# Attention and output projection of a band-attention layer, woven into one stage

## The chip, the core and the metric

One core of one Trainium2 chip runs the whole layer in one launch. The metric is the device time of that launch in microseconds (us). Engines that matter here: TensorE (PE: matmuls, and its weight loads, PEld), VectorE (DVE), ScalarE (ACT), GpSimd (POOL) and the DMA queues, nearly all of them issued by SyncE (SP). Each engine works through its own list of instructions in order; semaphores tie the lists together.

## The reference

All data is float32. 2048 prompt frames and 8 streams of 16 frames are projected by one matrix. One half of the channels goes through a gated MLP, the other through banded attention: 8 heads of 64 channels, queries in chunks of 64, each seeing its own chunk and the 8 before it, with a learned bias by clipped distance. Both halves are gated, multiplied by `w_out`, added to the input and normalised.

```python
def _band_attn_prompt(q, k, v, rel_table):
    ...
    scores = jnp.einsum('bnqhd,bnkhd->bnhqk', qc, kb).astype(jnp.float32) * (HEAD_DIM_B ** -0.5) + bias[None, None]
    scores = jnp.where(valid[None, :, None, None, :], scores, -jnp.inf)
    p = jax.nn.softmax(scores, axis=-1).astype(v.dtype)
    o = jnp.einsum('bnhqk,bnkhd->bnqhd', p, vb)
...
def _merge(x, a_out, z_a, b_out, z_b, w_out, g, bb):
    y = jnp.concatenate([a_out * jax.nn.silu(z_a), b_out * jax.nn.silu(z_b)], axis=-1)
    out = jnp.einsum('bse,ed->bsd', y, w_out)
    return _layernorm(ALPHA * x + out, g, bb)
```

## The kernel before

It has three stages, one after the other, with an end-of-block meeting of all engines between them.

1. **Input projection** (until about 700 us of the trace). The change leaves it alone but for small things named below. Each product is three float32r matmuls (high x high, high x low, low x high), which are nearly as exact as float32.
2. **Attention** (`attention`). The 2048 frames are 16 tiles of 128 queries. The outer loop runs over 4 pairs of heads, the inner over the 16 tiles: 64 units. A deep tile (number 4 and up, 12 of 16) sees 640 keys, which is 5 key tiles; tile 0 sees 1, tile 1 sees 2, and so on. A unit is a chain over three engines: PE makes the **scores** of both heads (L996; the low and high parts of a key stand on the two halves of the 128 rows, so two matmuls do a head's product); DVE adds the bias and finds the row's extreme (L921, one for each head); ACT takes the exponent and the row sum (L864); DVE **normalises** (reciprocal L928, scaling L930); PE **turns** the 128x128 blocks (L1006) into one of three PSUM banks; ACT copies them out (L872); PE **weighs** the values (L1019); DVE gates the sum (L940) into a store. PE's list has, at tile t, the scores of t, the weighing of t-2 and the turning of t-1. Meanwhile POOL splits `w_out` into its high and low parts, 8 pieces of 128x1024 (cast L854, subtraction L856), two for each pair of heads.
3. **Output projection** (`output_projection`). For each of 17 tiles of 128 rows (16 of the prompt, one of the 8 streams' frames): the gated activations come back from DRAM, ACT takes the high part (L1216), DVE the low part (L1255), PE makes two halves of 512 columns of 24 matmuls each (L1356), DVE adds the residual and takes statistics (L1264, L1267, L1273), POOL takes the root (L1203, L1205), DVE centres and scales (L1276, L1282), and the tile is stored. The 8 streams' small attention is threaded in, one stream every two tiles (L1365 to L1384).

Everything that PE writes has a bank of its own in stage 3: four banks for the output halves.

## Time and profile before

| | us |
|---|---|
| median of 3 runs | 1170.11 (1166.11 to 1170.15) |
| profiled execution, its own time | 1168.34 |
| its span, first to last instruction | 1166.3 |
| PE busy in the span | 1112.8 (95%) |
| stage 2 on PE, 704.2 to 956.4: PE busy | 221.3 of 252.2 |
| stage 3 on PE, 956.4 to 1158.8: PE busy | 201.7 of 202.4 |

The span is what the trace covers; the run's own time is 2.0 us longer, and the median of the runs another 1.8 us. PE's busy time counts each matmul until its modelled end, and matmuls overlap: how fast PE works is read from the distance of their starts. A row of the timeline has start, duration, engine, line, operation, what it writes and reads, and how many instructions are merged.

### The profile page before, as it was taken

Reading aid. Unit: us, or ns where it says so; the run is one execution under the profiler, and the core shown is the slowest. Engines: PE = TensorE matmul, PEld = TensorE weight load, DVE = VectorE, ACT = ScalarE, POOL = GpSimd, SP = SyncE. Lnnn points to the kernel's source line nnn. Section 1 sums busy time; section 2 is a strip of 40 time slices with the busy share of each in tenths; the row PEclk is TensorE's granted clock in tenths of the full one; section 3 lists DMA queues with packets and bytes.
Section 4 is the critical chain, followed back from the end, with each engine's and each line's share of the span. In section 5 each row is a group of like instructions: output and inputs, shape, how many; then the busy total and the mean of one; then the engine's idle time right before and its main releaser. Section 6 shows DMA issues by size and latency. Waiting matters only on the chain. (4 is left out here: it accounts for less than half of the span.)

```text
span 1166.3 us, 19127 instructions
## 1 busy us (share of the span) xinstructions
PE 1112.8 (95%) x6792; PEld 982.2 (84%) x6792; DVE 508.5 (44%) x1060; ACT 331.5 (28%) x690; POOL 93.4 (8%) x114
## 2 busy tenths in 40 slices
PE   6999999999999999999999995989898989999997
PEld 5999999999899999999999994878787877777775
DVE  4400112022222232222223225888888865665655
ACT  4411111111111111111111113768686761111110
POOL 0000000000000000000000010220202001111111
PEclk9999999999999999999999996999999999999999
DMA  8561111011342343244234339978787806545541
GB/s 275 184 193 64 55 38 56 26 66 43 120 155 81 109 148 115 93 139 144 76 109 152 110 97 226 272 193 197 188 197 179 198 29 201 164 127 158 161 135 72
DMA packets 127939, 155.81 MB, mean 134 GB/s; under 512 B 9097, under 2 KB 89121, under 8 KB 127905
## 3 DMA queue, kind: packets, MB, share of 16 engines
q1 hardware_dynamic: 123584, 139.63, 41.0%
q10 hardware_dynamic: 4320, 15.73, 4.2%
q8 instruction: 20, 0.33, 0.1%
q14 instruction: 15, 0.11, 0.0%
HBM read 101.56 MB, written 56.91 MB: 136 GB/s over the span
## 5 line engine op out<-in xcount | busy, mean ns | idle before, releaser
L601 PE MATMUL bank<-xh,wh 128*128 128x384 f32 (+1 forms) x1120 | 404.9, 362 | 9.4 <-DVE xl L487 7.9
L601 PE MATMUL bank<-xh,wl 128*128 128x384 f32 (+1 forms) x1120 | 401.1, 358 | 0.0
L601 PE MATMUL bank<-xl,wh 128*128 128x384 f32 (+1 forms) x1120 | 400.5, 358 | 0.0
L601 PEld LDWEIGHTS bank<-xh,wh 128*128 128x128 f32 x1120 | 211.0, 188 | 28.4 <-issue 9.1
L601 PEld LDWEIGHTS bank<-xh,wl 128*128 128x128 f32 x1120 | 210.8, 188 | 18.3
L601 PEld LDWEIGHTS bank<-xl,wh 128*128 128x128 f32 x1120 | 211.0, 188 | 17.5
L864 ACT ACTIVATE prob<-prob,low 128x640 f32<-128x640 f32 (+4 forms) x128 | 96.7, 756 | 66.2 <-DVE low L921 65.8
L1356 PE MATMUL out_ps<-wo_h,yh 128*128 128x512 f32 x272 | 109.5, 403 | 1.6 <-DVEq L1251 1.6
L1356 PE MATMUL out_ps<-wo_h,yl 128*128 128x512 f32 x272 | 106.3, 391 | 0.0
L1356 PE MATMUL out_ps<-wo_l,yh 128*128 128x512 f32 x272 | 106.1, 390 | 0.0
L514 DVE SCALAR_TENSOR_TENSOR st_b<-st_b,bank 128x384 f32<-128x384 f32 (+1 forms) x40 | 24.3, 607 | 181.0 <-ACT st_b L432 108.7
L1019 PE MATMUL o_ps<-pt,v 128*64 128x128 f32 x1120 | 77.5, 283 | 21.5 <-DVE st_b L940 14.4
L921 DVE CUSTOM_DVE_ANT_0 prob<-s_ps,bias 128x640 f32<-128x640 f32 (+4 forms) x128 | 90.0, 736 | 13.7 <-PE s_ps L996 10.6
L996 PE MATMUL s_ps<-k,q 128*128 128x320 f32 (+2 forms) x448 | 85.7, 331 | 8.3 <-DMA k<-s_k 8.2
L1019 PEld LDWEIGHTS o_ps<-pt,v 128*64 128x64 f32 x1120 | 61.7, 139 | 36.3 <-DVE st_b L940 16.8
L482 DVE TENSOR_TENSOR wl<-raw,wh 128x1024 fp32r<-128x1024 f32 x29 | 35.4, 1221 | 125.5 <-ACT wh L371 125.5
L567 DVE SCALAR_TENSOR_TENSOR st_b<-bank,st_a 128x384 fp32r<-128x384 f32 (+1 forms) x40 | 24.4, 611 | 144.2 <-ACT st_a L454 144.2
L930 DVE TENSOR_SCALAR prob<-prob,rden 128x640 f32<-128x640 f32 (+4 forms) x128 | 77.2, 603 | 4.5
L872 ACT ACTIVATE pt<-pt_ps 128x512 f32<-128x512 f32 (+1 forms) x168 | 75.8, 512 | 7.9 <-PE pt_ps L1006 7.8
L1006 PE MATMUL pt_ps<-ident,prob 128*128 128x128 f32 x560 | 77.6, 285 | 0.0
L996 PEld LDWEIGHTS s_ps<-k,q 128*128 128x128 f32 x448 | 68.8, 195 | 10.0 <-DMA k<-s_k 8.9
L1006 PEld LDWEIGHTS pt_ps<-ident,prob 128*128 128x128 f32 x560 | 62.4, 145 | 11.3 <-issue 11.3
(115 smaller groups left out, 818.0 us busy)
## 6 DMA issues: line engine op xcount, KB each, us to landing
raw<-w_all ACTq DMA_DIRECT2D x30, 512.0 KB, 3.3
q<-s_q SPq DMA_DIRECT2D x60, 256.0 KB, 6.0
par<-x SPq DMA_DIRECT2D x17, 512.0 KB, 3.3
big<-s_y SPq DMA_DIRECT2D x16, 512.0 KB, 5.3
y_out<-r SPq DMA_DIRECT2D x16, 512.0 KB, 3.1
k<-s_k SPq DMA_DIRECT2D x30, 256.0 KB, 7.2
big<-s_va SPq DMA_DIRECT2D x17, 256.0 KB, 3.3
big<-s_gate SPq DMA_DIRECT2D x17, 256.0 KB, 3.5
```

The source lines that it names most:

```text
L482: nc.vector.tensor_tensor(wl[s][:], raw[s][:], wh[s][:].bitcast(f32), ALU.subtract).then_inc(w_ready, 1)
L514: nc.vector.scalar_tensor_tensor(out=st, in0=st, scalar=1.0, in1=bank[c][:, 0:n], op0=ALU.add, op1=ALU.mult).then_inc(evac[c], 1)
L567: nc.vector.scalar_tensor_tensor(out=st_b[e % 2][:, 0:n].bitcast(f32r), in0=bank[c][:, 0:n], scalar=QSCALE if kind == "q" else 1.0, in1=st ...
L601: last = nc.tensor.matmul(bank[c][:, 0:width], w[s][:, kc, :], xx[:, kc, t0:t0 + width], start=kc == 0 and a == 0, stop=kc == KC - 1 and a ...
L864: nc.scalar.activation(prob[s][:, 0:n], prob[s][:, 0:n], ACT.Exp, bias=low[:, s:s + 1], scale=-1.0, accum_out=den[:, s:s + 1]).then_inc(ex ...
L872: nc.scalar.activation(pt[t % 2][:, 4 * e:4 * e + m, :], pt_ps[(BANKS[t] + e) % 3][:, 0:m, :], ACT.Copy).then_inc(pt_copied, 1)
L921: nc.vector.tensor_tensor_reduce(out=out, in0=src, in1=b, scale=1.0, scalar=MASKED, op0=ALU.add, op1=ALU.min, accum_out=low[:, s:s + 1]).t ...
L930: nc.vector.tensor_scalar(prob[s][:, 0:n], prob[s][:, 0:n], rden[:, s:s + 1], None, ALU.mult).then_inc(normed, 1)
L996: last = nc.tensor.matmul(s_ps[h][:, b, 0:m], q[:, h, part, t * P:(t + 1) * P], k[:, h, k0 + at:k0 + at + m], start=part == 0, stop=part == 1)
L1006: last = nc.tensor.transpose(pt_ps[(BANKS[t] + e) % 3][:, i - 4 * e, :], prob[(2 * t + h) % 4][:, b * P:(b + 1) * P], ident[:])
L1019: last = nc.tensor.matmul(o_ps[64 * h:64 * h + 64, 0:P], v[:, t + 1 - nk + b, 64 * h:64 * h + 64], pt[t % 2][:, 2 * b + h, :], start=b == ...
L1356: last = nc.tensor.matmul(out_ps[2 * s + h][:], y[s][:, c, :], w[:, c, 512 * h:512 * h + 512], start=c == 0 and a == 0, stop=c == KC - 1 a ...
```

## The change

Stages 2 and 3 become one stage, `attention_and_output`, written out in full (no loops). Its list is a sequence of 72 units: tile 0 with pairs 0 to 3, then stream 0, then tile 1 with its four pairs, then stream 1, and so on; from tile 8 on there are no streams left and a tile is four units. 81 steps run over it. In step s PE issues the scores of unit s, the turning of unit s-1 (first two groups of blocks), a **quarter** of a finished tile's output matmuls (12 of 48, in two lots of 6 with the third group of blocks between them), and the weighing of unit s-1. A tile's gating is one step after its last weighing, the high and low parts of its activations are taken in the same step, and its quarters follow. No quarter stands in steps 0 to 5 and in steps 10, 15, 20, 25, 30, 35 and 40; the stream tile is the ninth to be projected. The last 9 steps have no attention.

What else changes with it:

- The scores of a head pair are 12 matmuls instead of 8: three products (high x high, high x low, low x high), each over the 64 rows of its head alone, the two heads on rows 0 to 63 and 64 to 127 one after the other. Keys sit in a ring of 6 tiles, so 640 columns are two runs, of 384 and 256 or 512 and 128 columns.
- Turning has two PSUM banks instead of three, the output one bank (the very last half another) instead of four.
- Centring and scaling of 15 of the 17 output tiles go from two DVE instructions to three POOL instructions (L1025, L1028, L1030 of the new kernel). The last two tiles keep DVE's.
- The gated attention sums stay in SBUF, and gating is one instruction for a tile instead of four.
- The bias is loaded for all heads at the start of the stage (1.3 MB; before, the first 0.65 MB came during stage 1 and 0.65 MB more for each pair); queries are loaded once, not twice.
- POOL splits `w_out` in one run from the start of the stage.

```diff
+def output_schedule(order):
+    split, quarters, ends = [], {}, []
+    for k, tile in enumerate(order):
+        at = max(gate_step(tile), split[-1] if split else 0, ends[k - 2] + 1 if k > 1 else 0)
+        start = max(at + 1, ends[-1] + 1 if ends else 0)
+        for j in range(4):
+            quarters[start + j] = (k, j // 2, j % 2)
...
-                    for b, at, m in halves:
-                        for part in range(2):
-                            last = nc.tensor.matmul(s_ps[h][:, b, 0:m], q[:, h, part, t * P:(t + 1) * P],
-                                                    k[:, h, k0 + at:k0 + at + m], start=part == 0, stop=part == 1)
+                for first, count, at in runs:
+                    for i, (a, c) in enumerate(((0, 0), (0, 1), (1, 0))):
+                        for h in range(2):
+                            rows = slice(HD * h, HD * h + HD)
+                            last = nc.tensor.matmul(s_ps[h][:, at:at + count * P], q[t % 2][rows, a * GRP + p, :],
+                                                    k[rows, c * GRP + p, first * P:(first + count) * P],
+                                                    start=i == 0, stop=i == 2)
...
+            pool.wait_ge(par_loaded, 32)
+            for n in range(TILES):
+                root(n)
+                if n < POOL_TILES:
+                    pool.wait_ge(rstd_ready, n + 1)
+                    nc.gpsimd.tensor_scalar(r[n % 2], r[n % 2], mv[n % 2][:, 0:1], rstd[n % 2][:],
+                                            ALU.subtract, ALU.mult).then_inc(centred, 1)
+                    pool.wait_ge(centred, n + 1)
+                    nc.gpsimd.tensor_tensor(r[n % 2], r[n % 2], gain[:], ALU.mult).then_inc(scaled, 1)
+                    pool.wait_ge(scaled, n + 1)
+                    nc.gpsimd.tensor_tensor(r[n % 2], r[n % 2], offset[:], ALU.add).then_inc(r_ready, 1)
...
+            for step in range(STEPS):
+                if step < NU:
+                    if UNITS[step][0] == "stream":
+                        stream_scores(step)
+                    else:
+                        scores(step)
...
+                groups = turned_groups(step - 1) if 1 <= step <= NU else 0
+                for e in range(min(2, groups)):
+                    turn(step - 1, e)
+                if 2 <= step < NU + 2 and UNITS[step - 2][0] == "stream":
+                    turn_back(UNITS[step - 2][1])
+                if step in QUARTERS:
+                    n, h, part = QUARTERS[step]
+                    project(n, h, 4 * part, 4 * part + 2)
+                if groups > 2:
+                    turn(step - 1, 2)
+                if step in QUARTERS:
+                    project(n, h, 4 * part + 2, 4 * part + 4)
+                if 1 <= step <= NU:
+                    weigh(step - 1)
```

**PE, one deep unit.** Before, in the loop over tiles (the names: `s_ps` scores, `o_ps` weighed sums, `pt_ps` turned blocks):

```order
L996 MATMUL s_ps<-k,q 128x320 x4
L993 REGISTER_ALU
L996 MATMUL s_ps<-k,q 128x320 x4
L1015 REGISTER_ALU
L1016 REGISTER_ALU
L1019 MATMUL o_ps<-pt,v 64x128 x10
L1003 REGISTER_ALU
L1006 MATMUL pt_ps<-ident,prob 128x128 x4
L1003 REGISTER_ALU
L1006 MATMUL pt_ps<-ident,prob 128x128 x6
L993 REGISTER_ALU
L996 MATMUL s_ps<-k,q 128x320 x4
```

After, in a step of a deep tile (`out_ps` is the output half):

```order
L1255 MATMUL s_ps<-k,q 128x512 x6
L1255 MATMUL s_ps<-k,q 128x128 x6
L1288 MATMUL pt_ps<-ident,prob 128x128 x8
L1345 MATMUL out_ps<-wo_h,yh 128x512
L1345 MATMUL out_ps<-wo_l,yh 128x512
L1345 MATMUL out_ps<-wo_h,yl 128x512
L1345 MATMUL out_ps<-wo_h,yh 128x512
L1345 MATMUL out_ps<-wo_l,yh 128x512
L1345 MATMUL out_ps<-wo_h,yl 128x512
L1288 MATMUL pt_ps<-ident,prob 128x128 x2
```

The weighing has moved behind the turning of the same unit, a quarter of an output tile stands around the third group of blocks, and the scores are 12 matmuls of unequal widths. In a step without a quarter, the `out_ps` rows are absent.

**POOL, after the splitting of the weights.** Before, in stage 3, a tile (`rstd_o` is the root):

```order
L1197 MEMSET qd 128x128
L1207 UNCONDITIONAL_BRANCH
L1207 ISA
L1203 TENSOR_TENSOR rstd_o<-mv_o,eps 128x1
L1205 TENSOR_TENSOR rstd_o<-rstd_o,minus_half 128x1
L1207 REGISTER_ALU
L1207 COMPARE_AND_BRANCH
```

After, an output tile (`par` holds the rows to be normalised):

```order
L1015 TENSOR_TENSOR rstd_o<-mv_o,eps 128x1
L1017 TENSOR_TENSOR rstd_o<-rstd_o,minus_half 128x1
L1025 TENSOR_SCALAR par<-par,mv_o,rstd_o 128x1024
L1028 TENSOR_TENSOR par<-par,gain 128x1024
L1030 TENSOR_TENSOR par<-par,offset 128x1024
```

Three instructions over 128x1024 have come to POOL for each of 15 tiles.

**DVE, the step in which an output tile's last quarter ends, and the start of the next one.** Before, a deep unit of stage 2, where `low` is the row's extreme and `st_b` the gated tile:

```order
L921 ISA prob,low<-s_ps,bias 128x640
L921 ISA low 128x1
L914 REGISTER_ALU
L921 ISA prob,low<-s_ps,bias 128x640
L921 ISA low 128x1
L928 RECIPROCAL rden<-den 128x1
L930 TENSOR_SCALAR prob<-prob,rden 128x640
L928 RECIPROCAL rden<-den 128x1
L930 TENSOR_SCALAR prob<-prob,rden 128x640
L939 REGISTER_ALU
L940 SCALAR_TENSOR_TENSOR st_b<-o_ps,z 128x128
```

After (`yl` is the low part of the next tile's activations):

```order
L1179 BN_STATS stats_o<-par 128x6
L1188 BN_AGGR mv_o<-stats_o 128x2
L1146 SCALAR_TENSOR_TENSOR big<-o_ps,z 128x512
L1116 ISA prob,low<-s_ps,bias 128x640
L1116 ISA low 128x1
L1116 ISA prob,low<-s_ps,bias 128x640
L1116 ISA low 128x1
L1133 RECIPROCAL rden<-den 128x1
L1135 TENSOR_SCALAR prob<-prob,rden 128x640
L1133 RECIPROCAL rden<-den 128x1
L1135 TENSOR_SCALAR prob<-prob,rden 128x640
L1237 TENSOR_TENSOR yl<-big,yh 128x1024
```

The residual, the statistics, the gating of a whole tile and the taking of the low part have come between the biases and normalisations.

## Rows read from the trace of the kernel before

**Rows 1.** The page: busy PE, and its clock in 40 slices of 29.2 us.

```profile
PE 1112.8 (95%) x6792; PEld 982.2 (84%) x6792; DVE 508.5 (44%) x1060; ACT 331.5 (28%) x690; POOL 93.4 (8%) x114
...
PEclk9999999999999999999999996999999999999999
```

**Rows 2.** Windows, the stages on PE: busy us and counts by engine, clock, DMA share, GB/s.

```profile
704.20:956.40 252.20, 221.33 (x2140) 193.32 (x2140) 208.90 (x592) 175.72 (x426) 30.17 (x19) 0.95 0.76 188
956.40:1158.80 202.40, 201.67 (x1032) 157.37 (x1032) 120.71 (x204) 26.69 (x57) 26.21 (x33) 1.00 0.46 147
```

**Rows 3.** Timeline of PE, stage 2: a deep unit's period, then units of shallow tiles.

```profile
802.54 1.42 PE L996 MATMUL s_ps<-k,q 128*128 128x320 f32 x8
803.89 1.31 PE L1019 MATMUL o_ps<-pt,v 128*64 128x128 f32 x20
805.13 1.31 PE L1006 MATMUL pt_ps<-ident,prob 128*128 128x128 f32 x10
806.20 1.42 PE L996 MATMUL s_ps<-k,q 128*128 128x320 f32 x8
...
783.50 0.44 PE L1019 MATMUL o_ps<-pt,v 128*64 128x128 f32 x4
783.87 0.66 PE L1006 MATMUL pt_ps<-ident,prob 128*128 128x128 f32 x4
```

**Rows 4.** Timeline of PE: single matmuls of 384 and of 512 columns.

```profile
699.89 0.33 PE L601 MATMUL bank<-xh,wl 128*128 128x384 f32 x1
700.07 0.33 PE L601 MATMUL bank<-xh,wh 128*128 128x384 f32 x1
...
986.07 0.39 PE L1356 MATMUL out_ps<-wo_h,yl 128*128 128x512 f32 x1
986.47 0.45 PE L1365 MATMUL ss_ps<-kt,qd 128*32 128x144 f32 x8
986.85 0.50 PE L1356 MATMUL out_ps<-wo_h,yh 128*128 128x512 f32 x1
...
1157.67 0.39 PE L1356 MATMUL out_ps<-wo_h,yl 128*128 128x512 f32 x1
1157.89 0.39 PE L1356 MATMUL out_ps<-wo_h,yh 128*128 128x512 f32 x1
```

**Rows 5.** Timeline of DVE and POOL where POOL splits weights, at 748 us.

```profile
748.46 0.86 DVE L930 TENSOR_SCALAR prob<-prob,rden 128x640 f32<-128x640 f32 x1
749.14 2.41 POOL L856 TENSOR_TENSOR wo_l<-raw_o,wo_h 128x1024 f32 x1 [0.17 <-POOL wo_h L854]
...
749.43 2.48 DVE L930 TENSOR_SCALAR prob<-prob,rden 128x640 f32<-128x640 f32 x1
751.50 1.30 POOL L854 CAST wo_h<-raw_o 128x1024 f32 x1
...
755.81 0.55 DVE L930 TENSOR_SCALAR prob<-prob,rden 128x640 f32<-128x640 f32 x1
```

**Rows 6.** Waits of PE, 700 to 960 us: total, times, longest.

```profile
PE o_ps L1019 <- DVE st_b L940: 14.4, 15, 2.4
PE s_ps L996 <- DMA k<-s_k: 8.2, 2, 5.8
PE o_ps L1019 <- ACT pt L872: 5.0, 9, 1.2
```

**Rows 7.** Groups by line and form (L355 is stage 1): count, busy us, mean ns, idle before.

```profile
L921 DVE CUSTOM_DVE_ANT_0 prob<-s_ps,bias 128x640 f32<-128x640 f32 x96 | 75.3, 819 | 6.6 <-PE s_ps L996 4.5
L864 ACT ACTIVATE prob<-prob,low 128x640 f32<-128x640 f32 x96 | 78.9, 823 | 46.1 <-DVE low L921 46.0
L872 ACT ACTIVATE pt<-pt_ps 128x512 f32<-128x512 f32 x112 | 60.0, 580 | 5.1 <-PE pt_ps L1006 5.1
L355 POOL TENSOR_TENSOR rstd<-rstd,minus_half 128x1 f32<-128x1 f32 x16 | 8.9, 554 | 1.3
L1267 DVE BATCH_NORM_STATS2 stats_o<-r 128x6 f32<-128x512 f32 x34 | 23.6, 694 | 1.2
```

**Rows 8.** Timeline of PE: start of stage 2, and half the clock at 774.5 us.

```profile
704.22 1.09 PE L1046 MATMUL pt_ps<-ident,big 128*128 128x128 f32 x4 [3.47 <-PEq L129]
711.07 1.11 PE L996 MATMUL s_ps<-k,q 128*128 128x128 f32 x4 [5.76 <-DMA k<-s_k]
...
773.28 1.31 PE L1019 MATMUL o_ps<-pt,v 128*64 128x128 f32 x20 [1.86 <-DVE st_b L940]
774.52 2.33 PE L1006 MATMUL pt_ps<-ident,prob 128*128 128x128 f32 x10
```

More of the change, by code:

```diff
@@ new lines, with heads_of, turned_groups, before @@
+UNITS = unit_order()
+NU = len(UNITS)
+PLACE = {(kind, a, b): u for u, (kind, a, b) in enumerate(UNITS)}
+def heads_of(u):
+    return 2 if UNITS[u][0] == "pair" else 1
+def turned_groups(u):
+    kind, t, _ = UNITS[u]
+    return -(-2 * key_tiles(t) // 4) if kind == "pair" else 2
+def before(count):
+    out = [0]
+    for u in range(NU):
+        out.append(out[-1] + count(u))
+    return out
+HEADS_BEFORE = before(heads_of)
+GROUPS_BEFORE = before(turned_groups)
+STREAMS_BEFORE = before(lambda u: UNITS[u][0] == "stream")
@@ new lines, in gate_step @@
+def gate_step(tile):
+    return PLACE["pair", tile, GRP - 1] + 2 if tile < PTILES else PLACE["stream", SB - 1, None] + 2
+def output_schedule(order):
[5 more added lines that the diff above has]
+            quarters[start + j] = (k, j // 2, j % 2)
+        split.append(at)
+        ends.append(start + 3)
+    return split, quarters, ends
@@ L1210, in _ @@
         @block.scalar
         def _(act):
-            def high(n, s, loads):
-                act.wait_ge(y_loaded[s], loads)
-                act.wait_ge(out_done, n * 2 + 2)
-                nc.scalar.activation(yh[s][:], yr[s], ACT.Copy).then_inc(y_high, 1)
-            def step(i, last):
-                high(i * 2 + 1, 1, i * 16 + 16)
-                stream(i, 1)
-                stream(i, 2)
-                stream(i, 3)
-                if not last:
-                    high(i * 2 + 2, 0, i * 16 + 32)
@@ L1336, in _ @@
-            with dve.Fori(0, SB - 1) as i:
-                step(i, False)
-            step(SB - 1, True)
-            for h in range(2):
-                residual(PTILES, 0, h, 16 * (SB + 1), 16 * (SB + 1))
-            finish(PTILES, 0, parts=2)
+                for part in range(2):
+                    at = slice(D // 2 * part, D // 2 * (part + 1))
+                    nc.vector.scalar_tensor_tensor(out=r[n % 2][:, at], in0=r[n % 2][:, at], scalar=rstd[n % 2][:],
+                                                   in1=offset[:, at], op0=ALU.mult, op1=ALU.add).then_inc(last_ready, 1)
```

1078 lines of the change are left out of this document (516 added, 562 removed).

## The prediction

> **What bounds the kernel now.** I read the page's busy shares and clock line first [rows 1]: PE is busy 95% of the span, at full clock but for a dip around 700 us. The windows by stage [rows 2] then split what the change touches: stage 2 takes 252.2 us on PE with 221.3 busy, stage 3 takes 202.4 with 201.7 busy. Stage 3 has nothing to win on PE; stage 2 has some 31 us of idle PE and a little slow clock. So the weave can give back stage 2's gaps at most, by laying output matmuls into them.
>
> What those gaps are decides. The steady period of a deep unit is 3.66 us, from 802.54 to 806.20, and PE has no gap in it [rows 3]. The list of PE's waits [rows 6] puts 14.4 us on DVE's gating, 8.2 us on the loading of keys, 5.0 us on ACT's copies. The DVE gating is late where DVE itself has been held up: at 749.43 a normalisation lasts 2.48 us, against 0.55 us at 755.81, and it ends 0.36 us after POOL's subtraction, which ran from 749.14 to 751.55 [rows 5]. The earlier one lasts 0.86 us beside the cast. **A normalisation waits for a running POOL instruction, and then POOL waits for it** (the cast from 751.50 takes 1.30 us beside the end of it). POOL does this work four times in stage 2, and the fault is small. The Trainium skill (GPSIMD Engine Reference, Key points) says that POOL shares its SBUF interfaces with VectorE, with contention for DVE instructions in a 2-port mode or with two SBUF inputs; by that rule normalisations collide and bias additions, which read one operand from PSUM, don't, and the trace agrees.
>
> **PE's work after the change.** Output: 816 matmuls of 512 columns, 0.22 to 0.23 us apart [rows 4], 185 us, as before. Turning is unchanged, 1.07 us for 10 blocks (805.13 to 806.20). Weighing is 20 matmuls in 1.24 us and 4 in 0.37 us [rows 3]: 0.054 us each and 0.15 us besides, which is what a change from the full array to half-width matmuls costs. The scores of a deep unit take 1.35 us with such a change in it, 1.2 us without.
>
> The new scores use 64 of the 128 rows for each head. The trace has no matmuls on half the rows. It has half-width ones: 0.054 us apart for 128 columns, where turning needs 0.107 us for the same 128 columns; two heads go through the array side by side. Four quarter-width ones do so too: 8 of 144 columns fit with their changes between 986.07 and 986.85 [rows 4]. I take the same for half the rows, so 12 matmuls cost 6: three of 384 columns at 0.17 us [rows 4] and three of 256 at an estimated 0.12 us, 0.9 us. The bounds: 0.9 us, and 12 single ones at 1.8 us. The Trainium skill (TensorEngine Tiling (Array Packing), Key Properties) says that tiles operate independently and that a change of tiling mode drains the array; by it the scores cost 0.9 us and the step has one more change, which is what I take. In a step the shapes are half rows, full, half width: three changes of 0.15 us instead of two. Deep unit: 0.9 + 1.07 + 1.09 + 0.45 = 3.5 us against 3.66 us. Over 48 deep units that is -7 us; the 16 shallow ones gain nothing and pay a change each, +2.4. **Work: -5 us.**
>
> **PE's waits that go.** Stage 2 holds 48 x 3.66 = 176 us of deep units, about 32 us of shallow ones (8 for each pair of heads) and 2 for the stream tail of the MLP: 210 of 252.2 us. So 42 us are waits and slow clock; 2 us more lie in stage 3 (202.4 - 185 - 15 for eight streams at an estimated 1.9 us, of which the first insertion is 0.55 us, from 986.30 to 986.85 [rows 4]). All of it is taken out here, **-44 us**, and what the new stage waits for is put back.
>
> **Waits that come, a and b: start and first steps.** The first scores came at 711.07, 6.9 us after 704.22 [rows 8], for the keys. This stays. The bias now comes behind the first queries and keys: 1.3 MB at the 220 GB/s of that time is 6 us, with some of it beside the rest: +5. Then ten steps have little or no output work. Each is a chain: scores, bias and normalisation on DVE, exponent on ACT, turning, copy, weighing; for shallow tiles about 3.5 us without POOL. But POOL splits its 8 pieces in one run here, 3.5 us each [rows 5], so nearly every normalisation meets a cast or a subtraction: 5 us a step. PE's own work in them is 8 small units at 1.2 to 1.7 us, two streams and one tile's four quarters at 2.73 us, 26 us. Waits: 50 - 26 = 24 us. **a + b: 36 us.**
>
> **c and d: the output tiles' normalisation on POOL.** Take the step after a tile's last quarter, time 0 at its first score matmul. DVE ends the residual and statistics (0.7 us each [rows 7]) at about 1.5; root on POOL 0.75 (554 ns [rows 7] and a small one) to 2.3; the scaling by a pair of scalars, not in the trace, I price as the cast, 1.04 to 1.3 us: 3.5; two products of 2.4 us each like L856 [rows 5]: 5.9 and, with a normalisation let in between, 8.9. On the other side: scores end 1.2, both biases (0.82 us each [rows 7], 0.75 apart) end 2.7; ACT copies two groups (0.5 us each), exponent of head 0 ends 3.6, the third group's copy 4.2, exponent of head 1 at 5.1. Undisturbed, the second normalisation is done at 6.0, and PE wants it at 7.4, after quarter, weighing and next scores: 1.4 us to spare. Disturbed: normalisation 0 wants to start at 3.8, gets its turn at 5.9; the last product goes ahead; normalisation 1 starts at 8.9, ends 9.5. PE waits 2.1 us. **d:** this holds for 7 tiles (those ending at steps 44 to 68; behind the one that ends at 72 there is no attention): 15 us. **c:** 7 tiles end just before steps 10, 15, ... 40. The step behind them has no quarter, so PE comes for the blocks at about 4.5 us instead of 7.4 and waits 5; I take 4.3 each, since the pieces overlap a little: 30 us. **e:** a stream's placing on DVE that PE awaits, a new sum that waits for the gating, about 1 us for each of 8 streams, and one bank for both output halves in the last steps, 1 us: 9 us.
>
> **Sum, against the profiled execution's span:** 1166.3 - 5 - 44 + 36 + 30 + 15 + 9 = 1207.3; its own time is 2.0 us more, 1209.3, and the median of the runs lay 1.8 us above that. I say **1211 us, slower by 3.5%**. Hidden at no cost: the stage boundary that goes (it is in the 44); loads of 2.8 MB for each tile in 25 to 30 us, half of what the queues moved in stage 2 (188 GB/s [rows 2]); DVE's own load, 14 us of attention and 5 us of output in a plain tile's 25 us. SP's list waits in order for stores, but a store is due 1.5 steps after its tile. If DVE's cover is gone, d is what it costs.
>
> **Rivals.**
> 1. **PE absorbs the collisions: faster.** If POOL's three instructions start at other moments than in my timeline, or run shorter, each meets at most one normalisation, whose delay of up to 1.9 us is near the 1.4 us to spare. Then d goes, c shrinks to the 1 us that it has anyway, and b by 8: 1211 - 15 - 23 - 8 = 1165, and with half of e 1161. For it: DVE has 6 us of slack in a tile. Against: at 749 us a single run of POOL hit two normalisations in a row. Chance 0.17. Half absorbed: 1166 to 1195, chance 0.14.
> 2. **Half the clock.** At 774.52 turning takes 2.33 us instead of 1.31, after a gap of 1.86 us [rows 8]: the clock had gone from 2.4 to 1.2 GHz. Waits of 4 to 5 us in seven tiles and a dozen in the first ten steps could each be followed by a slow stretch at some 1 to 1.5 us: +15 to +20, 1228. For it: gap and slow stretch stand side by side; against: stage 2 had 15 waits on the gating [rows 6] and still a mean clock of 0.95 [rows 2]. Chance 0.12.
> 3. **Half-row matmuls don't go side by side.** Then scores cost 1.8 us: +0.9 x 48 = 43 us of work, of which some 20 us fall into the waits of c and d: 1235. Decides if the two heads' starts lie 0.17 us apart rather than a few ns. Chance 0.09.
> 4. The code written out in full is fetched from memory; no row has a price, the opening of stage 1 is written out as well and shows no such waits. No chance of its own.
>
> **The numbers.** Forecast 1195 to 1222: 0.48. With the rivals, 8 in 10 lie between 1160 and 1233: left out are a part of rival 1 and the upper parts of 2 and 3. About 0.5% is what a measurement of this kernel can tell from no change: 1164.3 to 1176.0. Faster than that: rival 1 nearly whole, 0.16; within: 0.08; slower: 0.76.
>
> **What would show it.** Right: normalisations of 2 to 3 us twice for each output tile, just where POOL has its 128x1024 instructions; gaps before PE's turning, 2 us from tile 8 on and 4 to 5 us before; the two heads' score matmuls starting within 10 ns. Wrong: normalisations all at 0.55 us beside busy POOL; steps of the deep tiles in 6.3 us throughout; PE gaps that end on DMA or on ACT's copies.

## The result, and the profile after

The changed kernel takes **1177.87 us** (four runs, 1175.74 to 1179.38) against 1170.11 us before: a ratio of 1.0073, 95% interval 1.0046 to 1.0101. It is slower, as forecast, but by 8 us, not by 41. In the series of the experiments, where the kernel before took 1166.6 to 1167.8 us, two versions that turned out to take the changed kernel's time, e4 and e9, stand at a ratio of 1.009. The profiled execution took 1179.38 us, with a span of 1177.7.

The page of the changed kernel, the rows that answer to [rows 1]:

```profile
PE 1116.0 (95%) x7040; PEld 962.9 (82%) x7040; DVE 488.2 (41%) x972; ACT 334.1 (28%) x689; POOL 219.0 (19%) x163
...
PEclk9999999999999999999999995799999999999999
```

Windows of the changed kernel, answering to [rows 2]: the **opening** (until the score matmuls of tile 2's second pair begin) and the rest until PE's last matmul. Columns: window and length, busy us (count) of PE, PEld (its weight loads), DVE, ACT, POOL, then the mean granted clock of PE as a share of full speed, DMA share, GB/s.

```profile
704.46:770.91 66.45, 40.68 (x245) 27.37 (x245) 34.01 (x97) 15.71 (x53) 32.25 (x27) 0.65 0.79 244
770.91:1169.94 399.03, 386.02 (x3175) 303.63 (x3175) 275.30 (x610) 189.45 (x431) 149.76 (x75) 1.00 0.35 107
```

PE's stretch from the start of the woven stage to its last matmul is 465.5 us; before it was 454.6 [rows 2]. So 10.9 of the 11.4 us that the span grew lie here. The rest of the stage is dense: 386.0 busy of 399.0, at full clock. The opening is not: 66 us, a mean clock of 0.65, the queues at 79%.

Waits of PE in the changed kernel, 704 to 1178 us, answering to [rows 6] (total, times, longest):

```profile
PE pt_ps L1288 <- DVE prob L1135: 9.7, 12, 2.2
PE o_ps L1364 <- DVE big L1095: 5.5, 1, 5.5
PE s_ps L1255 <- DMA k<-s_k: 4.8, 1, 4.8
...
PE s_ps L1267 <- DMA kt<-cache_k: 2.8, 1, 2.8
PE s_ps L1255 <- DVE low L1116: 2.0, 7, 0.4
PE out_ps L1345 <- DVE yl L1237: 1.9, 7, 0.6
```

The first row is where the prediction had 45 us of waiting (c and d) and a part of b. It is 9.7 us, and 4.9 of it fall into the opening: 4.8 us are left for all the tiles behind it. The groups say why (count, busy us, mean ns of one):

```profile
L1135 DVE TENSOR_SCALAR prob<-prob,rden 128x640 f32<-128x640 f32 x96 | 63.9, 666 | 3.4
L1025 POOL TENSOR_SCALAR par<-par,mv_o,rstd_o 128x1024 f32<-128x1024 f32 x15 | 57.2, 3813 | 1.6
...
L1028 POOL TENSOR_TENSOR par<-par,gain 128x1024 f32<-128x1024 f32 x15 | 38.3, 2554 | 1.3
L1237 DVE TENSOR_TENSOR yl<-big,yh 128x1024 fp32r<-128x1024 f32 x16 | 35.0, 2187 | 2.8 <-ACT yh L1081 2.8
```

POOL's centring and scaling (L1025) takes **3.81 us**, where the prediction had 1.04 to 1.3. The normalisations take 0.67 us in the mean, against 0.55 undisturbed. It is the low part of the activations on DVE (L1237) that has grown, from 1.22 to 3.39 us in seven tiles, and PE hardly waits for it.

The timeline of the changed kernel where a tile's last quarter is behind and the next step has none: DVE and POOL, start and duration.

```profile
851.33 3.85 POOL L1025 TENSOR_SCALAR par<-par,mv_o,rstd_o 128x1024 f32<-128x1024 f32 x1
852.93 0.55 DVE L1135 TENSOR_SCALAR prob<-prob,rden 128x640 f32<-128x640 f32 x1
853.74 0.55 DVE L1135 TENSOR_SCALAR prob<-prob,rden 128x640 f32<-128x640 f32 x1
854.49 1.23 DVE L1237 TENSOR_TENSOR yl<-big,yh 128x1024 fp32r<-128x1024 f32 x1 [0.19 <-ACT yh L1081]
855.27 2.74 POOL L1028 TENSOR_TENSOR par<-par,gain 128x1024 f32<-128x1024 f32 x1
857.82 0.55 DVE L1135 TENSOR_SCALAR prob<-prob,rden 128x640 f32<-128x640 f32 x1
858.09 2.53 POOL L1030 TENSOR_TENSOR par<-par,offset 128x1024 f32<-128x1024 f32 x1
859.12 1.85 DVE L1135 TENSOR_SCALAR prob<-prob,rden 128x640 f32<-128x640 f32 x1
```

While L1025 runs, both normalisations and the low part take their usual time. Here the products come when the step's two normalisations are done, and only the last one of the next step is hit (1.85 us), within PE's slack. In a plain tile (from tile 8 on, where every step has a quarter) it is closer:

```profile
1071.61 3.79 POOL L1025 TENSOR_SCALAR par<-par,mv_o,rstd_o 128x1024 f32<-128x1024 f32 x1
1074.66 1.08 DVE L1135 TENSOR_SCALAR prob<-prob,rden 128x640 f32<-128x640 f32 x1
1075.48 2.50 POOL L1028 TENSOR_TENSOR par<-par,gain 128x1024 f32<-128x1024 f32 x1
1075.67 3.39 DVE L1237 TENSOR_TENSOR yl<-big,yh 128x1024 fp32r<-128x1024 f32 x1
```

The second normalisation takes 1.08 us and ends 0.26 us after the product's start, and the low part waits for the product. Of the 96 normalisations of 128x640, 24 begin beside L1025: 17 took 0.55 or 0.56 us, and seven, one in each of the plain tiles and all at its end as here, took 0.93 to 1.08. Why these seven ran long is open: at 0.55 us each would have ended before the product began.

### The profile page after: what moved, and what is told of

Its sections match the earlier page's. It is cut to its first block and busy times, and to the rows that moved or that the text cites. A ratio compares the mean times of both kernels' runs of the same rounds, so it can differ in the third digit from the quotient of the medians.

```text
span 1177.7 us, 18220 instructions
## 1 busy us (share of the span) xinstructions
PE 1116.0 (95%) x7040; PEld 962.9 (82%) x7040; DVE 488.2 (41%) x972; ACT 334.1 (28%) x689; POOL 219.0 (19%) x163
## 5 line engine op out<-in xcount | busy, mean ns | idle before, releaser
L1043 ACT ACTIVATE pt<-pt_ps 128x512 f32<-128x512 f32 (+1 forms) x168 | 82.2, 524 | 181.7 <-PE pt_ps L1288 178.6
L1345 PE MATMUL out_ps<-wo_h,yh 128*128 128x512 f32 x264 | 114.9, 435 | 4.7 <-DVE yl L1237 1.9
L1051 ACT ACTIVATE prob<-prob,low 128x640 f32<-128x640 f32 (+3 forms) x136 | 101.1, 745 | 24.4 <-DVE low L1116 24.4
L1135 DVE TENSOR_SCALAR prob<-prob,rden 128x640 f32<-128x640 f32 (+4 forms) x136 | 93.3, 686 | 4.8
L1288 PE MATMUL pt_ps<-ident,prob 128*128 128x128 f32 x560 | 85.0, 283 | 9.7 <-DVE prob L1135 9.7
L1116 DVE CUSTOM_DVE_ANT_1 prob<-s_ps,bias 128x640 f32<-128x640 f32 (+1 forms) x112 | 85.4, 800 | 19.8 <-PE s_ps L1255 19.6
L1255 PE MATMUL s_ps<-k,q 64*128 64x256 f32 (+3 forms) x696 | 72.2, 338 | 6.9 <-DMA k<-s_k 4.8
L330 POOL TENSOR_TENSOR rstd<-mv,eps 128x1 f32<-128x1 f32 x16 | 3.0, 190 | 378.9 <-DVE mv L512 378.9
```

Source lines behind the costliest of these rows:

```text
L1043: nc.scalar.activation(pt[u % 2][:, 4 * e:4 * e + m, :], pt_ps[group % 2][:, 0:m, :], ACT.Copy).then_inc(pt_copied, 1)
L1051: nc.scalar.activation(prob[s][:, 0:n], prob[s][:, 0:n], ACT.Exp, bias=low[:, s:s + 1], scale=-1.0, accum_out=den[:, s:s + 1]).then_inc(ex ...
L1116: nc.vector.tensor_tensor_reduce(out=out, in0=src, in1=b, scale=1.0, scalar=MASKED, op0=ALU.add, op1=ALU.min, accum_out=low[:, s:s + 1]).t ...
L1135: nc.vector.tensor_scalar(prob[s][:, lo:n], prob[s][:, lo:n], rden[:, s:s + 1], None, ALU.mult).then_inc(normed, 1)
L1255: last = nc.tensor.matmul(s_ps[h][:, at:at + count * P], q[t % 2][rows, a * GRP + p, :], k[rows, c * GRP + p, first * P:(first + count) * ...
L1288: last = nc.tensor.transpose(pt_ps[group % 2][:, i - 4 * e, :], prob[slot(u, h)][:, lo + b * P:lo + (b + 1) * P], ident[:])
```

## Experiments

Ratios are to the kernel before, measured in turn with it on the same chip; its median there was 1166.6 to 1167.8 us. The changed kernel itself stood at 1.0073. The middle column is the median; windows and waits are from one profiled execution of each.

| | us | ratio | 95% interval |
|---|---|---|---|
| e1 all tiles finished on DVE | 1221.2 | 1.0464 | 1.0442 to 1.0487 |
| e2 short first POOL instruction | 1211.7 | 1.0395 | 1.0371 to 1.0418 |
| e5 e2, products after the normalisations | 1203.1 | 1.0305 | 1.0274 to 1.0337 |
| e10 e5, and after the low part | 1177.2 | 1.0086 | 1.0060 to 1.0112 |
| e3 no low part of w_out | 1171.7 | 1.0044 | 1.0029 to 1.0058 |
| e4 filler for the clock | 1177.8 | 1.0092 | 1.0075 to 1.0110 |
| e6 splitting on ACT and DVE | 1183.1 | 1.0140 | 1.0114 to 1.0165 |
| e7 order of loads | 1172.1 | 1.0046 | 1.0030 to 1.0062 |
| e8 e6 and e7 | 1170.0 | 1.0029 | 1.0016 to 1.0042 |
| e11 e8, finer | 1165.4 | 0.9983 | 0.9969 to 0.9998 |
| e12 e11 and filler | 1166.1 | 0.9989 | 0.9976 to 1.0002 |
| e9 heads one after the other | 1178.1 | 1.0090 | 1.0058 to 1.0122 |
| e13 both heads on the same rows | 1241.6 | 1.0634 | 1.0598 to 1.0671 |
| e14 e11, products held back | 1164.1 | 0.9977 | 0.9964 to 0.9990 |
| e15 e14, a quarter spread | 1164.1 | 0.9965 | 0.9952 to 0.9977 |

### Do POOL's instructions cost anything? (e1)

```diff
-TAIL = 2
+TAIL = TILES
...
-                    if ENDS[n] + 3 == step and n < POOL_TILES:
-                        sp.wait_ge(r_ready, n + 1)
+                    if ENDS[n] + 2 == step and n < TILES - 2:
+                        sp.wait_ge(last_ready, 2 * n + 2)
```

> The changed kernel, with centring and scaling of all 17 output tiles on DVE (as its last two have it); POOL keeps only the two small instructions of the root and the splitting of w_out. Theory 1, the opening is the loss: in the changed kernel PE's waits on normalisations are 9.7 us in all, 4.9 of them before 772 us, so POOL's centring and products cost the end nothing; 1174 to 1180 us against 1177.9, deep steps still 6.35 us. Theory 2, that of the prediction (POOL's products hold up normalisations and PE waits for them): whatever they cost goes, at most the 4.8 us of the later waits on normalisations and 1.9 us on the low part, 1170 to 1173.

It took 1221.2 us, 43 us more, so both theories fall. DVE's finish of a tile stands in its list ahead of the next unit's bias. The timeline of e1, DVE:

```profile
1022.68 1.29 DVE L1194 SCALAR_TENSOR_TENSOR par<-par,mv_o,gain 128x1024 f32<-128x1024 f32 x1
1024.49 1.42 DVE L1200 SCALAR_TENSOR_TENSOR par<-par,rstd_o,offset 128x512 f32<-128x512 f32 x2 [0.52 <-POOL rstd_o L1017]
1025.82 0.68 DVE L1146 SCALAR_TENSOR_TENSOR big<-o_ps,z 128x512 f32<-128x512 f32 x1
1026.42 0.81 DVE L1116 CUSTOM_DVE_ANT_1 prob<-s_ps,bias 128x640 f32<-128x640 f32 x1
```

The scores for that bias began at 1021.51. In the step before, without a finish, the bias came 1.3 us after its scores (1016.44 and 1015.16); here it is 4.9. Exponent, copies and PE's weighing follow: in each of seven plain tiles PE waited some 1.8 us for ACT's copies (12.3 in all), and in the seven steps without a quarter 23.2 us. That POOL takes this work is worth some 43 us against this placing, collisions and all; a finish behind the unit's biases in DVE's list was not tried.

### The length of one instruction (e2, e5, e10)

```diff
-                    nc.gpsimd.tensor_scalar(r[n % 2], r[n % 2], mv[n % 2][:, 0:1], rstd[n % 2][:],
+                    nc.gpsimd.tensor_scalar(r[n % 2][:, 0:1], r[n % 2][:, 0:1], mv[n % 2][:, 0:1], rstd[n % 2][:],
```

> The changed kernel, with POOL's first instruction for an output tile (subtract mean, times root; 3.8 us in the trace, priced at 1.04 to 1.3 in the prediction) cut to one column of 1024, so the output isn't centred and scaled. The two products behind it then start 3.7 us earlier, about where the prediction's timeline had them. Theory 1, PE absorbs what collisions there are: 1174 to 1180 us, PE's waits on normalisations stay near 10 us. Theory 2, the long first instruction is what moved the products out of the way: PE waits 2 us in each tile from 8 on and 4 us in each of seven tiles before, together up to 45 us, 1190 to 1222.

**1211.7 us**: cutting POOL's work by 51 us made the kernel 34 us slower, and theory 2 holds. The same place as above, in e2:

```profile
861.41 2.39 POOL L1028 TENSOR_TENSOR par<-par,gain 128x1024 f32<-128x1024 f32 x1
862.54 1.61 DVE L1135 TENSOR_SCALAR prob<-prob,rden 128x640 f32<-128x640 f32 x1
863.88 2.46 POOL L1030 TENSOR_TENSOR par<-par,offset 128x1024 f32<-128x1024 f32 x1
864.25 2.44 DVE L1135 TENSOR_SCALAR prob<-prob,rden 128x640 f32<-128x640 f32 x1
```

Each product now meets a normalisation, which ends after it. The second is done 7.5 us after its step began (at 859.24); in the changed kernel it was 4.7 us (854.29 after 849.63). PE's waits on normalisations in e2 behind 771 us:

```profile
PE pt_ps L1288 <- DVE prob L1135: 27.2, 14, 3.8
```

The step behind the one without a quarter took 12.48 us instead of 7.68 in the tile shown, 4.8 more: the wait, and a mean clock of 0.73 in that step. Seven such steps lost 34.6 us (4.5 to 5.4 each). Plain tiles lost 0.3 to 0.5 us each (a step of 6.99 instead of 6.54), 3 in all, and the opening was 3.5 us shorter than the changed kernel's (62.95). The windows behind the opening tell how the loss divides:

```profile
766.02:1202.24 436.22, 403.21 (x3175) 318.96 (x3175) 286.76 (x610) 189.85 (x431) 91.22 (x74) 0.94 0.32 98
```

37.2 us more than the changed kernel's 399.03 with the same 3175 matmuls: 20.0 are idle PE (33.0 against 13.0), and 17.2 are PE busy for longer at the lower clock.

Is it the moment of the products, or something else in the long instruction?

```diff
                     pool.wait_ge(centred, n + 1)
+                    pool.wait_ge(normed, HEADS_BEFORE[min(ENDS[n] + 2, NU)])
```

> As e2_short_scale (the first POOL instruction of an output tile cut to one column of 1024, output not centred and scaled), and POOL waits before its first product until both normalisations of the step behind the tile's last quarter are done. In e2 both products ran into both of them (1.4 to 1.7 us and 2.4 to 2.5 us instead of 0.55) and the step after the one without a quarter took 12.2 to 12.7 us instead of 7.7. Theory 1, the moment at which the products start is what decides: the 4.8 us a tile go, 1174 to 1180 us, about as the changed kernel. Theory 2, something else in the long first instruction mattered (its own time on POOL, the clock): stays at 1200 to 1212.

1203.1 us, which neither theory gave. The plain tiles lost nothing any more (6.36 us throughout), but the steps behind those without a quarter took 10.5 to 12.6 us. The timeline of e5:

```profile
864.71 2.37 POOL L1029 TENSOR_TENSOR par<-par,gain 128x1024 f32<-128x1024 f32 x1 [2.73 <-DVE prob L1136]
864.76 3.41 DVE L1238 TENSOR_TENSOR yl<-big,yh 128x1024 fp32r<-128x1024 f32 x1 [0.20 <-ACT yh L1082]
867.16 3.26 POOL L1031 TENSOR_TENSOR par<-par,offset 128x1024 f32<-128x1024 f32 x1
```

The normalisations are clear, but product and low part start together. The low part waits for the product (2.37 us and its own 1.2), the next product for the low part, and the next bias and PE's quarter stand behind the low part: PE waited 17 us for it, and some 13 us more are slow clock (399.6 us busy behind the opening, against 386.0). So POOL was made to wait for the low part too:

```diff
                     pool.wait_ge(normed, HEADS_BEFORE[min(ENDS[n] + 2, NU)])
+                    pool.wait_ge(y_split, n + 2)
```

> As e5_short_wait (short first POOL instruction, products of an output tile held back until the normalisations of the step are done), and held back too until DVE has made the low part of the next tile's activations. In e5 all tiles' low parts took 3.16 to 3.42 us instead of 1.22, since product and low part started together, and seven tiles still lost 4 to 5 us, the others nothing. Theory, the moment decides and the low part was the second instruction hit: the seven steps fall from 11.4 to 12.6 us to about 7.7: 1174 to 1178. Rival, the long first instruction helps in another way: stays near 1203.

**1177.2 us**, the changed kernel's time, with POOL's work 51 us less. The product starts at 854.18, 0.2 us after the low part's end in that tile (852.78 and 1.23 us), against 855.27 beside 854.49 in the changed kernel. Behind the opening e10 takes 398.9 us, the changed kernel 399.0. That settles it: the moment decides, and the slow first instruction had kept the products out of the way by chance. One thing the edit doesn't do: in the plain tiles the low part beside the product is that of the tile after next, the new wait is met before, and the low parts still took 3.4 us (at 1022.17, the product at 1022.11). It costs nothing there (steps of 6.35 us).

The Trainium skill (SBUF — State Buffer, Who interferes with whom) says that two SBUF inputs on DVE, or one of its 2-port modes, contend with a GpSimd instruction, and that the one issued first holds the shared ports to its end. For products against normalisations and low parts the traces agree (2.44 and 3.41 us). For the POOL instruction with two per-partition scalars they do not: 17 of 24 normalisations beside it took 0.55 us, the other seven 0.93 to 1.08 at its end, and seven low parts 1.22 to 1.23.

### The opening (e3, e4, e6, e7, e8, e11, e12)

In the opening the prediction's mechanism is at work. The changed kernel, DVE and POOL:

```profile
722.07 2.34 POOL L1005 TENSOR_TENSOR wo_l<-gain,wo_h 128x1024 fp32r<-128x1024 f32 x1
722.18 2.32 DVE L1135 TENSOR_SCALAR prob<-prob,rden 128x128 f32<-128x128 f32 x1
```

A normalisation of 0.29 us takes 2.32. How much of 66 us is that?

```diff
-                nc.gpsimd.tensor_tensor(wo_l[at], raw_o[g % 2], wo_h[at].bitcast(f32), ALU.subtract).then_inc(wo_done, 1)
+                one = (slice(None), slice(0, 1), slice(g * P, g * P + 1))
+                nc.gpsimd.tensor_tensor(wo_l[one], raw_o[g % 2][:, 0:1, 0:1], wo_h[one].bitcast(f32),
+                                        ALU.subtract).then_inc(wo_done, 1)
```

> The changed kernel without the low part of w_out: POOL's subtraction of each piece is cut to one column, and PE multiplies the high part in its place, so PE's work is the same and the products miss the low part. POOL then splits 8 pieces in 1.04 us each instead of 3.4. Theory 1, the opening is the loss and POOL's splitting a part of it: the three normalisations of 2.3 to 2.4 us and the one of 1.4 before 738 us fall to 0.3 (some 7 us), pieces are there earlier; 1166 to 1172 us. Rival, the opening is bound by transfers (queues 85% busy from 711 to 750 us): 1174 to 1178.

1171.7 us: 6 us less, as theory 1 had it. The opening lasted 58.4 us (703.99 to 762.39). The clock was tried next, by filler:

```diff
+            def fill(count):
+                for _ in range(count):
+                    nc.tensor.matmul(out_ps[:], ident[:], wts[:].rearrange("p g t -> p (g t)"), start=True, stop=True)
...
+            fill(4)
...
+                fill({0: 5, 1: 1, 2: 2, 3: 2, 4: 1, 5: 1}.get(step, 0))
```

> The changed kernel with 16 matmuls of no use (identity times 512 float32 columns, into the output bank before its first use) put into PE's waits of the first seven steps. Theory 1, half clock: it ran at half clock from 703.7 to 748.1 us; with PE busy the clock stays at 2.4 GHz, and the 11 us of work at full clock that stand there save up to 8 us: 1169 to 1173. Theory 2, what ends the waits there is transfers and POOL's splitting, PE's speed is hidden: 1175 to 1179, the granted clock higher and the 770 us mark where it was.

Theory 2 holds. Windows of e4 and of the changed kernel over the same stretch:

```profile
704.46:750.00 45.54, 35.28 (x169) 19.76 (x168) 20.25 (x70) 10.75 (x40) 25.89 (x18) 0.85 0.92 284
```

```profile
704.46:750.00 45.54, 24.46 (x134) 15.98 (x134) 24.06 (x65) 10.52 (x36) 25.17 (x22) 0.52 0.89 275
```

The clock goes from 0.52 to 0.85, the time stays (1177.8 us), and the score matmuls of step 11 begin at 770.61 instead of 770.91: PE at half speed was hidden behind transfers and POOL's chain. Moving the splitting alone, and the loads alone:

```diff
+                if step < KC:
+                    act.wait_ge(raw_o_loaded[step % RAW], 16 * (step // RAW + 1))
+                    nc.scalar.activation(wo_h[:, :, step * P:step * P + P], raw_o[step % RAW], ACT.Copy).then_inc(wo_high, 1)
...
+                if step < KC:
+                    at = (slice(None), slice(None), slice(step * P, step * P + P))
+                    dve.wait_ge(wo_high, step + 1)
+                    nc.vector.tensor_tensor(wo_l[at], raw_o[step % RAW], wo_h[at].bitcast(f32),
+                                            ALU.subtract).then_inc(wo_done, 1)
```

> The changed kernel with the splitting of w_out off POOL: in each of the first 8 steps ACT takes the high part of a piece (1.04 us) after its exponents and DVE the low part (1.22 us) after its normalisations. e3 (no subtraction) was 6 us faster than the changed kernel. Theory 1, POOL's subtractions cost the opening by colliding with normalisations, and ACT and DVE have room there: 1168 to 1173 us. Rival: two buffers for the raw pieces and 5 to 7 us for each transfer make ACT and DVE wait in their lists, exponents and normalisations with them: 1177 to 1187.

The rival: 1183.1 us. With pieces landing late, what stands behind them in ACT's and DVE's lists waits too. Waits of PE in e6's opening:

```profile
PE s_ps L1264 <- DVE qd L1150: 5.4, 1, 5.4
...
PE o_ps L1320 <- ACT pt L1033: 4.8, 4, 2.0
```

```diff
-            load_qk(0)
-            near = skewed(s_skew, slice(0, HEADS), P, WIN - P, WIN)[:, :, WIN - NEAR:WIN]
-            sp.dma_start(bias[:, 2 * NEAR:].rearrange("p (h j) -> p h j", h=HEADS), near).then_inc(bias_loaded, 16)
-            load_qk(1)
+            load_qk_first((0, 1))
+            load_bias(0, 1)
...
+            load_qk_first((1, GRP))
+            load_wo(0)
+            load_bias(1, GRP)
+            load_wo(1)
```

> The changed kernel with the loads of its opening in another order, splitting left on POOL: queries, keys and bias of the first pair of heads alone come first, the rest behind them; four buffers for raw pieces of w_out instead of two; the second stream's keys before the last pieces; POOL takes the stream tile's root before it masks the bias. Theory 1, transfers bound the opening beside POOL: first scores 2 to 3 us earlier, first step's sum 3 to 5 us earlier, 2.8 us of waiting for the stream's keys go: 1167 to 1172 us. Rival, POOL's chain of splits and its collisions bound it: 1174 to 1177.

1172.1 us, just above theory 1's 1172 at most; POOL's collisions stayed. Both together:

> Both edits: e7's order of loads and e6's splitting on ACT and DVE. Theory, the opening is the whole loss: 16.4 MB in 69 us at some 330 GB/s leave 20 us to win, steps 0 to 5 take 2.6 us each instead of 3 to 8: 1157 to 1165 us, faster than the kernel before. Rival, queues carry what they can (91% busy from 704 to 748 us): 1167 to 1171.

1170.0 us, the rival: the queues were full from 708 to 745 us (335 GB/s, against 317 in the changed kernel), so the order of what they carry is what is left. The finer order:

```diff
+            load_first(0)
...
+            load_v(0)
+            load_first(1)
+            load_wo(0)
+            load_first(2)
+            load_wo(1)
+            load_first(3)
+            load_keys(0)
+            load_wo(2)
...
+PIECE_STEPS = {1: [0], 2: [1], 3: [2], 4: [3], 5: [4], 6: [5, 6], 7: [7]}
```

(`load_first(p)` brings queries, keys and bias of pair p.)

> e8_open_both with its loads in finer order: queries, keys and bias of the four pairs of heads one pair after the other with the raw pieces of w_out between them, what isn't needed before the first output quarters behind, the streams' bias issued by ACT, and the splitting of a piece in steps 1, 2, 3, 4, 5, 6, 6, 7 instead of 0 to 7. In e8 transfers ran at 99% from 708 to 745 us and step 6 began at 735.3. By 7.3 MB at 330 GB/s it can begin at 730. Theory, transfers bound the opening: 1162 to 1167 us. Rival, ACT and DVE waiting in their lists for pieces: 1169 to 1173.

1165.4 us, 12 us less than the changed kernel and barely below the kernel before. The opening of e11:

```profile
703.03:756.01 52.98, 39.40 (x245) 26.10 (x246) 33.67 (x105) 23.98 (x61) 5.39 (x14) 0.68 0.98 305
```

53.0 us instead of 66.5, the same 245 matmuls, the queues at 98% and 305 GB/s. 13.5 us gained in the opening and 14.1 in the span (1163.6): the loss against the kernel before lay in the opening.

> e11_open3 and 24 matmuls of no use (identity times 256 float32 columns) in PE's waits of the first seven steps. In e4 such matmuls raised the clock from 0.50 to 0.84 between 704 and 748 us and won nothing, since transfers and POOL's chain set the pace there. Theory: with these shorter, PE at half clock is late in step 6 (12 output matmuls took 5.3 us instead of 2.7): 2 to 4 us faster than e11. Rival: transfers still set the pace: the same as e11.

The rival again: clock 0.90 in the opening instead of 0.68, and 1166.1 us, no difference that can be measured.

### The heads side by side (e9, e13)

```diff
-                    for i, (a, c) in enumerate(((0, 0), (0, 1), (1, 0))):
-                        for h in range(2):
+                    for h in range(2):
+                        for i, (a, c) in enumerate(((0, 0), (0, 1), (1, 0))):
```

> The changed kernel with the score matmuls of the two heads issued one head after the other instead of alternately, nothing else. Theory (the prediction's reading): two matmuls on opposite halves of the 128 rows go side by side only if they follow each other; one head after the other, the 12 matmuls of a deep unit take some 1.8 us instead of the 1.07 us measured, 0.75 us more in each of 48 deep units and about half of that in 16 shallow ones: 1177.9 + 40 = 1210 to 1220 us. Rival: the time of a score matmul is set by something else and the order doesn't matter: 1176 to 1180.

1178.1 us: the order is without effect, and the theory falls as put. The single records show matmuls starting in pairs 10 ns apart, where they were 3 ns apart, three times in a row for 384 columns. A record doesn't name its head, but matmuls on the same rows start 0.17 us apart (e13), so a pair is read as one matmul of each head. What does matter are the rows:

```diff
-                            rows = slice(HD * h, HD * h + HD)
+                            rows = slice(0, HD)
```

> The changed kernel with both heads' score matmuls on rows 0 to 63, so that head 1's scores are made from head 0's queries and keys; nothing else. Theory (the prediction's): what makes 12 score matmuls of a deep unit cost 1.07 us is that the heads stand on different rows; on the same rows they take 1.8 us or more: 0.75 us more in 48 deep units and half of it in 16 shallow ones, 1210 to 1222 us. Rival: half-row matmuls cost this little whatever their rows: 1176 to 1180.

1241.6 us, more than either. The timelines of PE in e9 and in e13, a deep unit's 12 score matmuls (one row) and what follows:

```profile
1060.88 1.15 PE L1255 MATMUL s_ps<-k,q 64*128 64x384 f32 x12
1061.96 1.10 PE L1288 MATMUL pt_ps<-ident,prob 128*128 128x128 f32 x8
```

```profile
1113.41 2.02 PE L1255 MATMUL s_ps<-k,q 64*128 64x384 f32 x12
1115.37 1.09 PE L1288 MATMUL pt_ps<-ident,prob 128*128 128x128 f32 x8
```

On the same rows they take 1.96 us from start to start, on different rows 1.08: side by side is worth 0.88 us a deep unit, 42 us in 48 of them and some 8 us in the 16 shallow ones. The other 14 us lie in five steps behind those without a quarter. One of them in the windows of e13:

```profile
862.96:875.47 12.51, 11.97 (x55) 9.59 (x55) 8.43 (x15) 5.39 (x13) 7.55 (x3) 0.59 0.46 154
```

PE was busy for 11.97 of 12.51 us there, at a mean clock of 0.59, for the most part at 1.2 GHz; the five took 10.6 to 12.5 us, where 7.7 and the 0.9 of the scores were due. What brought the clock down there was not tried.

### A version that beats both (e14, e15)

> e11_open3 with the fifth to eighth piece of w_out split in steps 6, 6, 7, 7 instead of 5, 6, 6, 7 (in e11 the fifth stood ahead of the first tile's low part on DVE, and PE waited for that), and with e10's waits, but POOL's first instruction whole: products of a tile start after the step's normalisations and the next tile's low part. Theory: 2 to 3 us from the opening, and the four deep steps of 6.55 us and DVE's low parts of 3.39 us go back to 6.35 and 1.22, worth 1 us: 1161 to 1164 us. Rival: POOL comes later by its waits and the second product meets the next normalisation: 1166 to 1170.

1164.1 us, just above the forecast's 1164 at most: the opening lasted 50.2 us, the low parts took 1.23 us in the mean, and plain steps 6.36. In plain tiles that is again a matter of moments, not of the wait: the low part began 0.2 us ahead of the product (1008.03 and 1008.25), and the product waited. Twelve normalisations took 2.0 to 2.5 us instead, and PE did not wait for them.

```diff
+for n in range(TILES - 1):
+    if ENDS[n] + 1 not in QUARTERS:
+        LOTS[ENDS[n]] = (n, 6, 1)
+        LOTS[ENDS[n] + 1] = (n, 7, 1)
+        ENDS[n] += 1
```

> e14 with the last quarter of a tile that has a stream behind it split over two steps, 6 output matmuls in the step that had 12 and 6 in the step that had none, so that no step is without output work. Steps of that kind and the one behind lose some 1.5 us to waits in each of seven tiles (gaps of 0.40, 0.22, 0.66 and 0.22 us). Theory: those gaps are latency that output work covers: 5 to 8 us faster than e14, 1154 to 1158. Rival: the gaps move to the step that has 6 matmuls less: within 2 us of e14.

The rival: 1164.1 us. The waits moved. In e14 PE waited nine times for normalisations behind the opening, 5.1 us in all; in e15 it waits for the low part instead:

```profile
PE out_ps L1372 <- DVE yl L1262: 10.9, 7, 1.6
```

Both are faster than the kernel before, by 0.2 and 0.35%, and than the changed one by about 1%. Most of it is e11's opening.

## Why the prediction was off

The direction held. The size was off by 33 us: 1177.87 lies outside the forecast of 1195 to 1222 and inside the range given for 8 in 10, 1160 to 1233. The sum of the prediction put PE's stretch at 495.6 us (454.6 and its terms, 41); it was 465.5. By its steps:

- **The waits that go (-44)** held: none of them came back behind the opening.
- **Work (-5)** came as +3.7. By the prediction's terms 405.6 us of work were due (454.6 - 44 - 5), 26 of them in the first ten steps and 379.6 behind; PE was busy for 388.3 us behind them. The deep step takes 6.36 us, not 3.5 + 2.73 = 6.23, and 6.44 to 6.50 where the keys' ring splits 640 columns into 512 and 128. The scores came at 1.07 us with their change, as priced (0.9 and 0.15). Timeline of PE:

```profile
1063.07 1.14 PE L1255 MATMUL s_ps<-k,q 64*128 64x384 f32 x12
1064.14 1.10 PE L1288 MATMUL pt_ps<-ident,prob 128*128 128x128 f32 x8
...
1069.43 0.44 PE L1255 MATMUL s_ps<-k,q 64*128 64x384 f32 x2
```

- **a + b (36)** was 37.4: from the start of the stage to the scores of step 10 (704.46 to 767.78) it took 63.3 us where the prediction had 61.9 (6.9, 5 and ten steps of 5). The mechanism named, POOL's splitting on top of transfers, was right; e3 puts 6 us on POOL's subtractions, e11 13 on both. Not foreseen: in the order of the queue the second stream's keys stand behind the last pieces of `w_out` (2.8 us of waiting).
- **c (30) and d (15)** were 4.8 together. This is the step that failed, and in it one number: "the scaling by a pair of scalars, not in the trace, I price as the cast, 1.04 to 1.3". It took 3.81 us. The timeline built on it put the first product at 3.5 us of its step; in the changed kernel it came at 6.05 (1075.48, the step from 1069.43), beside the end of the second normalisation.
- **e (9)** was 8.5: 2.9 on ACT's copies for a stream, 2.0 on the biases, 1.9 on the low part, 1.7 on the output bank.

3.7 - 44 + 37.4 + 4.8 + 8.5 = 10.4 of the 10.9 us measured.

e2 makes the instruction short (0.38 us), and the kernel takes 1211.7 us, where the prediction said 1211. The collisions came as described, but the agreement in size is luck. **c** and **d**, priced at 45 us of waiting, came as 27.2 us of waiting and 17.2 of slow clock, which the sum left to rival 2. The second normalisation was done 8.0 us into a plain tile's step, not 9.5, so **d** was 0.6 us a tile at most, not 2.1. Work was 9 us longer than priced, the first ten steps (59.8 us instead of 61.9) and e 2 us shorter each.

Of the rivals, the first is what happened. It named the condition, "if POOL's three instructions start at other moments than in my timeline", and the 1 us a tile that it left of c, 7 in all, is near the 4.8 measured. But its 1165 us took 8 us off the opening, which didn't come, and had the work some 9 us too short. That 1177.9 lies within its "half absorbed: 1166 to 1195" is no merit of that range: the collisions behind the opening were absorbed nearly whole. The second, half the clock, came in the opening and cost nothing there (e4, e12); it costs where PE has no slack (17 us in e2, and the long steps of e13). The third didn't come: 0.88 us a unit (priced 0.9) is what e13 measured for it, and 14 us more by the clock.

The fault of method was this. For an operation without a row the prediction took the nearest row by what it does (a cast, one input), and kept both ends close together. POOL's two-input row, 2.4 us [rows 5], was at hand, and with it the first product starts at 4.7 us of the step, when by the same timeline the first normalisation, due at 3.8, has gone free; the second, due from about 5.4 to 6.0, would still have met it. So that end would have taken a part of c and d away, and only a longer instruction the whole. A result that hangs on which of two engines comes first is a step, not a slope: more of the chance belonged to its other side.

## What to carry over

Two engines that block each other turn a schedule into a matter of moments: before pricing such a change, vary the duration of each unseen instruction in the timeline and see whether a collision appears or goes; if it does, both outcomes need their share. Then make the order explicit (a wait on the other engine's semaphore, e10) rather than leave it to a slow instruction, and read from the trace for every tile whether the wait does hold: the one for the low part in e10 and e14 did so in seven of 15. And price a woven stage's opening first: here it cost 37 us of the 44 that the weaving gave back, and 13 of them were a matter of who issues and splits what in which order. Where a forecast and a run agree in time, look at what the time is made of: 1211 and 1211.7 us were not the same sum.

## What the runs showed of the hardware

- A POOL instruction with one tensor and two per-partition scalars takes longer than one with two tensors: 3.81 us against 2.39 us undisturbed for 128x1024 float32. The Trainium skill (GPSIMD Engine Reference, Engine selection) has POOL at roughly line rate with one input and about 2 times slower than VectorE with two; among these POOL instructions the one with one tensor is the slower.
- Normalisations on DVE run beside that instruction at full speed (0.55 us in 17 of 24; the seven at its end took up to 1.08), and wait for products and subtractions to end (up to 2.5 us). Bias additions, which read one operand from PSUM, took 0.81 to 0.82 us beside all of them.
- Matmuls on rows 0 to 63 and on 64 to 127 run side by side even when three of the one are issued ahead of three of the other: starts 10 ns apart in e9, 1.08 us a unit (1.07 in the changed kernel, 1.96 on the same rows in e13). The Trainium skill (TensorE: Matmul & The Clock Gate, The mechanism) says that matmuls start and end strictly in order; the records of e9, read as above, speak against that for the starts of matmuls on different rows.
- With 16 matmuls more in the opening, PE's granted clock was 0.85 instead of 0.52 over 45 us, and the time was the same: there transfers and POOL's chain were what the rest waited for. Where PE had no slack, behind the opening of e2, the same 3175 matmuls kept it busy for 403.2 us instead of 386.0 at a mean clock of 0.94.
